# A transformer block's three FFNs: the gate and up products as Strassen's seven quarter products

## The reference, cut to what matters

```python
FFN_HIDDEN = -(-8 * D_MODEL // (3 * 256)) * 256          # 2816

def swiglu(h, w_in, w_out):
    gate, up = jnp.split(h @ w_in, 2, axis=-1)
    return (jax.nn.silu(gate) * up) @ w_out
```

## Time and profile before

| | |
|---|---|
| median of 3 runs | 1612.1 us |
| span of the profiled execution, first to last instruction | 1607.1 us |
| median less this span (what lies around it, and the difference of executions) | 5.0 us |
| TensorE busy | 1596.4 us, 99% |
| VectorE busy | 849.0 us, 53% |
| ScalarE busy | 502.5 us, 31% |
| mean granted TensorE clock | 0.997 |

### The profile page before, as it was taken

One profiled execution on the slowest core, in us unless ns is written; L12 is line 12 of the kernel. 1 busy time (PEld: TensorE's weight loads), 2 busy tenths in 40 slices (PEclk: granted clock), 3 DMA queues, 4 the chain that ended last, 5 costly groups with the idle time before them and its releaser, 6 DMA issues.

```text
span 1607.1 us, 19314 instructions
## 1 busy us (share of the span) xinstructions
PE 1596.4 (99%) x7785; PEld 1343.6 (84%) x7785; DVE 849.0 (53%) x1050; ACT 502.5 (31%) x589; POOL 119.9 (7%) x106
## 2 busy tenths in 40 slices
PE   9999999999999999999999999999999999999998
PEld 7888888888888888888888888888988888888887
DVE  5898764664433344584454444346456544444444
ACT  4554375522222233442222223221323222222222
POOL 0100000020000000000000003135006000000000
PEclk9999999999999999999999999999999999999999
DMA  9544511222222123322222223342212322222332
GB/s 388 193 156 159 208 53 53 80 79 96 87 104 104 66 89 98 116 79 105 99 84 104 91 73 105 98 146 103 80 53 79 105 104 94 89 104 69 95 100 77
DMA packets 30647, 171.35 MB, mean 107 GB/s; under 512 B 3200, under 2 KB 5504, under 8 KB 17152
## 3 DMA queue, kind: packets, MB, share of 16 engines
q1 hardware_dynamic: 26240, 153.80, 27.4%
q0 software_dynamic: 4352, 16.78, 3.1%
HBM read 168.47 MB, written 2.10 MB: 106 GB/s over the span
## 4 chain that ended last, share of the span: by engine, by line
PE 99%; issue 0%; DVE 0%; POOL 0%; ACT 0%; POOLq 0%; DVEq 0%
PE bank L515 98%; PE bank L814 0%; PE bank L870 0%; POOL root L420 0%; PE bank L738 0%; PE bank L1143 0%; DVE y_ffn L2534 0%; ACT tmp L1500 0%; POOLq L123 0%; DVE qd L2111 0%; DVE kd L2111 0%; DVE tmp L2091 0%; DVE y_ffn L2532 0%; ACT mod_rows L1289 0%; DVEq L123 0%
## 5 line engine op out<-in xcount | busy, mean ns | idle before, releaser
L515 PE MATMUL bank<-a_hi,w_all 128*128 128x512 f32 x2490 | 764.7, 390 | 0.0
L515 PEld LDWEIGHTS bank<-a_hi,w_all 128*128 128x128 f32 x2490 | 466.5, 188 | 98.8 <-issue 2.5
L1712 DVE TENSOR_TENSOR w_all<-w_raw,w_all 128x2048 fp32r<-128x2048 f32 x140 | 323.3, 2309 | 360.5 <-ACT w_all L1265 360.3
L515 PE MATMUL bank<-a_lo,w_all 128*128 128x512 f32 x1245 | 477.1, 389 | 0.0
L1265 ACT ACTIVATE w_all<-w_raw 128x2048 fp32r<-128x2048 f32 x142 | 271.7, 1913 | 562.7 <-PE bank L515 562.7
L515 PE MATMUL bank<-g_hi,w_all 128*128 128x512 f32 (+1 forms) x1088 | 331.9, 386 | 0.0
L515 PEld LDWEIGHTS bank<-a_lo,w_all 128*128 128x128 f32 x1245 | 233.7, 188 | 48.8 <-issue 0.5
L515 PEld LDWEIGHTS bank<-g_hi,w_all 128*128 128x128 f32 x1088 | 203.9, 189 | 41.2
L515 PE MATMUL bank<-g_lo,w_all 128*128 128x512 f32 (+1 forms) x544 | 210.2, 386 | 0.0
L515 PEld LDWEIGHTS bank<-g_lo,w_all 128*128 128x128 f32 x544 | 102.5, 188 | 20.6
L515 PE MATMUL bank<-w_all,a_hi 128*128 128x512 f32 (+1 forms) x384 | 108.9, 359 | 0.0
(11 more groups left out here) (289 smaller groups left out, 1339.3 us busy)
## 6 DMA issues: line engine op xcount, KB each, us to landing
w_raw<-in_ffn_in SPq DMA_DIRECT2D x66, 1024.0 KB, 4.8
w_raw<-in_ffn_out SPq DMA_DIRECT2D x24, 768.0 KB, 4.2
mod_raw<-in_mod POOLq DMA_DIRECT2D x16, 1024.0 KB, 5.6
w_raw<-in_ffn_out SPq DMA_DIRECT2D x24, 640.0 KB, 3.9
w_raw<-in_gla_in SPq DMA_DIRECT2D x10, 1024.0 KB, 5.1
w_raw<-in_mix_in SPq DMA_DIRECT2D x10, 1024.0 KB, 4.7
mod_w<-in_mod SPq DMA_DIRECT2D x8, 1024.0 KB, 18.4
w_raw<-in_gla_out SPq DMA_DIRECT2D x4, 1024.0 KB, 4.7
```

The lines of the kernel that those rows point to most:

```text
L515: return pe.matmul(out, lhs, rhs, start=first, stop=last, skip_group_check=True)
L1712: V.tensor_tensor(flat(w_lo[s]), flat(w_raw[s]), flat(w_hi[s]).bitcast(F32), ALU.subtract).then_inc(lo_done[s], 1)
```

## The change

In each FFN the first pair stays as it was. Pairs 2 to 11 (called pairs 1 to 10 of the combined form below, n = 1 to `LAST` = 10) are computed as seven quarter products in place of eight (Strassen's block product in the form with shared sums). The depth of 1024 is cut into two halves, the 256 columns of a unit into two chunks of 128, the 512 tokens into two halves of 256. A quarter product is 128 features x 256 tokens over a depth of 512; gate and up are done side by side in one bank. Seven sums of weight quarters (slots 0 to 6, three of them plain quarters, four by VectorE: `weight_first_two`, `weight_second`, `weight_fourth`) meet seven sums of token quarters (`xc`, made once per FFN, four by VectorE: `token_sums`). Each slot is split into upper and lower part (`weight_hi` on ScalarE, `weight_lo` on VectorE, 128 x 1024 each), each token sum likewise (`token_hi`, `token_lo`). The tokens are scaled by the norm's gains and roots before the sums (`tokens`).

TensorE does the seven products in the order of `STEPS`, 24 matmuls of 256 columns each. Products 0, 2 and 4 build up bank 0, and ScalarE copies the bank after each (`part_copy`) before the next may add to it; product 1 goes to bank 1, 3 and 6 to bank 2, 5 to bank 3. VectorE adds copy and bank to each quarter of gate and up (`quarter_sum`, four per pair; product 6 waits for the first of them), ScalarE applies Silu, VectorE multiplies (`hidden_product`). The hidden values' upper and lower parts are made later, at the end of the last pair and in the first quarter of the output stage.

The loads fill one raw buffer `w_pair` (2 MB for gate and up) by halves of the depth, 1 MB each: the first half for pair n+1 when four lower parts of pair n are done, the second when all seven are.

The diff's core (renamed semaphores, memory places and repeated forms left out):

```diff
+STEPS = ((0, 0, True), (6, 1, True), (5, 0, False), (1, 2, True), (4, 0, False), (2, 3, True), (3, 2, False))
...
+                for n in range(1, LAST + 1):
+                    before = N_STEPS * (LAST * f + n - 2)
+                    for half in range(2):
+                        if n > 1:
+                            sp.wait_ge(combo_lo, before + (4, N_STEPS)[half])
+                        w = slice(half * UNIT // 2, (half + 1) * UNIT // 2)
+                        to = w_pair[:, :, KD // 2 * half:KD // 2 * (half + 1)].rearrange("p u k c -> p u (k c)")
+                        sp.dma_start(to, w_in[CPU * n:CPU * (n + 1), :, w].rearrange("u p w -> p u w")).then_inc(half_in[half], 16)
...
+                def combined(first=False):
+                    for n, (x, b, begins) in enumerate(STEPS):
+                        pe.wait_ge(combo_lo, cnt.next(combo_lo))
+                        if first:
+                            pe.wait_ge(x_lo, cnt.next(x_lo))
+                            if n == 0:
+                                pe.wait_ge(gate_free, cnt.next(gate_free, CPU))
+                            if n == 3:
+                                pe.wait_ge(up_free, cnt.next(up_free, CPU))
+                        if n in (0, 2, 4) and (n or cnt.has(part_copied)):
+                            pe.wait_ge(part_copied, cnt.next(part_copied) if n else cnt.now(part_copied))
...
+                        if n == N_STEPS - 1:
+                            pe.wait_ge(c_added, cnt.next(c_added))
+                        for u in range(CPU):
+                            out = bank[b][:, u * TC:(u + 1) * TC]
+                            for k in range(KD // 2):
+                                m = mm3(out, (slot[n][:, 0, u, k], slot[n][:, 1, u, k]), (xc_hi[:, k, x], xc_lo[:, k, x]),
+                                        begins and u == 0 and k == 0, k == KD // 2 - 1)
...
+                def first_combined():            # ScalarE
+                    for which in range(3):
+                        part_copy(f, 1, which)
+                        weight_hi(f, 1, 4 + which)
+                        token_hi(f, 4 + which)
+                    weight_hi(f, 2, 0)
+                    gate_silu_of(f, 1, 1)
+                    for j in (1, 2, 3):
+                        weight_hi(f, 2, j)
+                    gate_silu_of(f, 1, 0)
+                    for j in (4, 5, 6):
+                        weight_hi(f, 2, j)
+                def combined(n):                 # ScalarE
+                    part_copy(f, n, 0)
+                    weight_hi(f, n + 1, 0)
+                    weight_hi(f, n + 1, 1)
+                    part_copy(f, n, 1)
+                    weight_hi(f, n + 1, 2)
+                    weight_hi(f, n + 1, 3)
+                    part_copy(f, n, 2)
+                    weight_hi(f, n + 1, 4)
+                    gate_silu_of(f, n, 1)
+                    weight_hi(f, n + 1, 5)
+                    weight_hi(f, n + 1, 6)
+                    gate_silu_of(f, n, 0)
...
+            def weight_first_two(f, n):          # VectorE
+                i = LAST * f + n
+                dve.wait_ge(half_in[0], ONCE + 16 * i)
+                V.tensor_tensor(quarter(4, n), raw_quarter(0, 0), raw_quarter(0, 1), ALU.subtract).then_inc(early_sums, 1)
+                dve.wait_ge(early_sums, 2 * i - 1)
+                dve.wait_ge(half_in[1], ONCE + 16 * i)
+                V.tensor_tensor(raw_quarter(0, 1), raw_quarter(0, 1), raw_quarter(1, 1), ALU.add).then_inc(early_sums, 1)
...
+                def combined(n):                 # VectorE
+                    weight_lo(f, n + 1, 0)
+                    weight_first_two(f, n + 1)
+                    weight_lo(f, n + 1, 1)
+                    weight_second(f, n + 1)
+                    weight_lo(f, n + 1, 2)
+                    weight_lo(f, n + 1, 3)
+                    quarter_sum(f, n, 1, 1)
+                    quarter_sum(f, n, 1, 0)
+                    weight_lo(f, n + 1, 4)
+                    quarter_sum(f, n, 0, 0)
+                    weight_lo(f, n + 1, 5)
+                    weight_fourth(f, n + 1)
+                    hidden_product(f, n, 1)
+                    quarter_sum(f, n, 0, 1)
+                    weight_lo(f, n + 1, 6)
+                    hidden_product(f, n, 0)
+                def last_combined():             # VectorE
+                    for k in range(CPU):
+                        hidden_lower(f, k)
+                    split_lo(0, width(0))
+                    quarter_sum(f, LAST, 1, 1)
...
+                weight_lo(f, 1, 0)
+                weight_lo(f, 1, 1)
+                if f == 1:
+                    dve.wait_ge(roots_copied, cnt.next(roots_copied))
+                elif f == 2:
+                    x_roots(5, False)
+                tokens()
+                token_lo(f, 0)
+                if scaled:
+                    first_gate()
+                token_lo(f, 1)
+                first_combined()
```

More of the change, by code:

```diff
@@ L935, in ahead_products @@
                     pe.wait_ge(ahead_lo, at + 1)
-                    m = mm3(bank[b][:], weights(0, k, 0), (g_hi[:, at], g_lo[:, at]), first and i == 0, last and k == AHEAD[-1])
+                    m = mm3(bank[b][:], weights(0, k, 0), (g_hi(at), g_lo[:, at]), first and i == 0, last and k == AHEAD[-1])
                 return m
@@ new lines, in quarter_sum @@
+            def quarter_sum(f, n, c, half):
+                i = LAST * f + n - 1
+                to = cbuf[:, :, c, HALVES[half]]
+                which, b, after = {(1, 1): (2, 2, 4), (1, 0): (2, 1, 2), (0, 0): (0, 3, 6), (0, 1): (1, 2, 7)}[c, half]
+                dve.wait_ge(part_copied, 3 * i + which + 1)
+                dve.wait_ge(product_out, N_STEPS * i + after)
+                if cnt.has(hidden):
+                    dve.wait_ge(hidden, cnt.now(hidden))
+                V.tensor_tensor(to, dec_k[which][:].rearrange("p (u t) -> p u t", u=CPU),
+                                bank[b][:].rearrange("p (u t) -> p u t", u=CPU), ALU.add).then_inc(c_added, 1)
```

617 lines of the change are left out of this document (375 added, 242 removed).

## The result

| | median of runs | ratio to before, 95% interval |
|---|---|---|
| before | 1610.5 us (1608.0 to 1613.7) | |
| after | 1676.1 us (1675.6 to 1677.2) | 1.0406, 1.0388 to 1.0425 |

The change costs 4.1%. The forecast was 1662 us, slower with a chance of 0.88. The direction and the mechanism came out as forecast; the time is 14 us longer. By spans it is 1674.5 against 1607.1: 67.4 us more, where 50.6 were forecast. The 5.0 us that the forecast added between span and median came to 1.6.

The account below looks back on a forecast made before the run. TensorE, busy 99% of the span, was taken to bound the kernel. Span 1607.1 - 48.0 saved + 98.6 of added waits = 1657.7, plus 5.0 to the median gives 1662 us; costs give 1650 to 1690, widened to 1632 to 1700.

Parts of the forecast that it names:

- The 5.0 us that the forecast added: Whole time: the median of runs lies 5.0 us above the profiled span, so this was added to 1657.7.
- TensorE's saving: Combined pairs: 20.16 us in place of 21.76 at 0.120 us per 256-column matmul, 48.0 us saved over 30 pairs.
- not some 99: Whole changed profile: TensorE idle some 99 us, named after VectorE's lower parts and a ScalarE bank copy.
- (a): Ahead of product 0 of pair 1: TensorE waits for work piled on VectorE, 4.8, 9.8 and 11.3 us per FFN.
- (b): Within pair 1: weights and token sums are split while TensorE works on it; waits 7.5, 9.8 and 9.8 us.
- (c): Within pair 2: product 2 waits 11.2 us for ScalarE's first copy of bank 0; 13.3 per FFN with later products.
- (d): Within pair 10: product 6 waits 1.85 us per FFN, as VectorE splits output weights ahead of the quarter sum.
- a load of 6.0 as its upper bound: Half loads in 4 KB rows to two places: taken as 4.8 us; at 6.0 the forecast grows by 24.
- nothing to spare: Pairs 3 to 9: the raw buffer loop takes 19.9 to 20.1 us, just under TensorE's 20.16.
- The second rival: Steady pairs: the raw buffer loop binds, 1 us more per pair in 24 to 27 pairs, 1680 to 1700; chance 0.13.
- I count nothing: Half clock behind the larger waits: priced at zero, since another wait follows that TensorE reaches anyway.
- the third rival: Behind the four larger waits per FFN: half-clock stretches, none hidden, cost 12 x 1.7 = 20 us, 1683; chance 0.10.

Follow-up runs that it names:

- rows_8k: Kernel after with each half load of a combined pair's weights in one 8 KB row per partition in place of two of 4 KB: 1664.5 us, 1.0336.
- rephase: Kernel after with the weight operations of pair n moved behind the sums of pair n-1, beside pair n itself instead of a pair ahead: 1628.3 us, 1.0110.
- plain_second: rephase with the second pair of each FFN also done plain, so 27 combined pairs in place of 30: 1577.0 us, 0.9788.
- copy_early: Kernel after with ScalarE's first copy of bank 0 in pair 2 issued right behind the upper part of slot 1: 1674.3 us, 1.0390.
- sum_early: Kernel after with VectorE's first quarter sum in pair 10 put ahead of its split of the first output unit: 1669.1 us, 1.0366.
- filled_waits: Kernel after with matmuls whose results nobody reads run in the four long waits of each FFN: 1678.5 us, 1.0421.

## Why the prediction was right, and what it mis-sized

TensorE's saving came out in its size: matmuls of 256 columns are spaced 0.120 us, a pair without waits takes 20.16 us (rows_8k, rephase). The waits stand where they were said to be, though the longest are named after the gate's banks and after copies, not after `slot` and `xc_lo`. TensorE idles 76.7 us more than before, not some 99, and is busy 1587.1 us in place of 1548: part of the lost time is work at half clock.

(a) The forecast had 25.9 us, the trace has 23.7 by the same row of VectorE. plain_second shows it causally: with 21.8 us of plain products beside the token work nearly all of it goes.

(b) The first FFN's product 6 starts 24.8 us behind product 0, as forecast; in the others 29.0 and 28.9 in place of 27.1, by the half clock behind product 2 (see below). Product 6 itself then takes 4.1 to 5.3 us, partly at half clock, in place of 2.9. That is why pair 1 is 2.3 to 3.1 us longer than forecast and pair 2 up to 1.8 shorter: the second pair's end is set by VectorE and the loads. From product 6 of pair 1 to the end of pair 2 it is 36.9, 36.7 and 37.4 us, where 36.3 were forecast.

(c) 8.7 to 9.5 us before product 2, where 11.2 were forecast; the half clock of product 6 takes part of it. The mechanism stands, but the name in the text was only its last link: "ScalarE's row has all seven upper parts of pair 2 ahead of the first copy" is true and can be undone without any gain (copy_early). What holds is the phase, weights of n + 1 ahead of the sums of n (rephase: -36.5 us in pair 2, -48 with the loop and (d) together).

(d) As forecast, 1.8 us three times.

The load. The forecast took 4.8 us from rows of 8 KB and gave a load of 6.0 as its upper bound. The page has 5.2 for the two rows of 4 KB, and rows_8k brings it back. That is 5.4 us in pairs 3 to 9; the prediction's mark for them, not over 20.5 us, was kept in the mean (20.42) and passed by a few pairs (up to 20.64). The prediction's sentence that the loop has "nothing to spare" was the right warning. The second rival came in by a fifth of the size it was given.

The clock. "I count nothing" is the term that was mis-sized most: it held for a part of the stretches, and the others cost some 12 us, where the third rival had 20.

Between product 0 and product 2 of pair 1 it held. This takes 9.2 us in the first FFN and 10.8 in the others, in the kernel after, copy_early, sum_early, rows_8k, filled_waits and rephase, at a granted clock anywhere from 0.67 to 1.00.

Behind product 2 of pair 1 it did not hold in the second and third FFN. The first 8 us from the start of product 2, in the second FFN of the kernel after, the third of rows_8k and the second of filled_waits:

```profile
756.46:764.46 8.00, 8.00 (x45) 8.00 (x46) 6.98 (x9) 4.24 (x5) 0.00 (x0) 0.63 0.40 133
...
1318.56:1326.56 8.00, 8.00 (x54) 8.00 (x55) 7.84 (x10) 4.24 (x5) 0.00 (x0) 0.79 0.37 131
...
756.71:764.71 8.00, 7.72 (x62) 7.54 (x63) 7.93 (x10) 4.25 (x5) 0.00 (x0) 1.00 0.41 131
```

From product 2 to product 6 it is 18.2, 17.0 and 16.0 us in these three. In the second and third FFN of the same six kernels, twelve places, it goes by the clock in the same way: 16.0 to 16.1 us at a clock of 1.00, 17.0 at 0.79 or 0.80, 18.1 to 18.2 at 0.62 to 0.64. So the kernel after loses 2.1 us in each of these two FFNs.

Outside of the combined pairs the traces before and after run nearly the same matmuls, and they drift apart only in stretches at half clock. Three of these, each before and then after the change: in the first mixer, in the first FFN's norm and in the second FFN's norm.

```profile
178.60:182.20 3.60, 3.52 (x21) 3.21 (x22) 3.56 (x4) 0.74 (x2) 0.00 (x0) 1.00 1.03 418
178.80:182.40 3.60, 3.60 (x13) 2.87 (x12) 2.49 (x2) 0.00 (x0) 0.00 (x0) 0.53 1.01 383
...
321.00:327.90 6.90, 6.90 (x49) 6.90 (x48) 5.62 (x13) 1.29 (x2) 3.51 (x3) 0.75 0.00 0
322.10:329.00 6.90, 6.90 (x35) 6.90 (x35) 4.99 (x11) 0.17 (x1) 3.26 (x4) 0.51 0.00 0
...
691.60:698.40 6.80, 6.80 (x30) 5.63 (x31) 6.46 (x13) 1.45 (x2) 1.21 (x2) 0.75 0.43 154
707.80:714.70 6.90, 6.90 (x24) 6.03 (x24) 5.54 (x11) 0.72 (x1) 1.41 (x2) 0.51 0.49 135
```

The first two bring the first pair's end 3.1 us later (353.0 in place of 349.9), the third costs 1.6. The fourth stands behind the wait on the roots in the third FFN, which lies in the midst of the up unit. There no second wait takes it up at once:

```profile
1296.50:1301.50 5.00, 5.00 (x10) 3.28 (x11) 2.25 (x4) 0.60 (x1) 0.00 (x0) 0.50 0.00 0
```

These 5 us at 0.50, the lower level of 1.2 GHz, behind a wait of 3.53 us cost 2.5 us of work (2.8 with what is left behind them), and the matmuls that spread the roots, which VectorE waits for, took 2.07 us for two in place of 1.02. The four together are 7.5 of the 7.9 us outside of the pairs; the rest is the difference between the matmuls' starts and their modelled ends.

Only the fourth is shown to come from the change, by its wait. The first three stand in work that the change hardly touches, and kernels with the same work there have them or not: sum_early is without the one in the mixer and ends the first pair 1.6 us earlier than the kernel after; rephase is without it, has half of the second, as the kernel before, and ends the first pair at 350.0. The runs of the kernel before differ in the same sense, from 1608.6 us at a mean clock of 0.997 to 1613.9 at 0.994. Its traced execution was one of the fast ones: a time lies about 1.8 us above its own span, and the rest of the 5.0 us that the forecast added was the distance from this execution to the median. Whether the change makes such stretches more frequent is open, with one trace of the kernel before and no experiment on them.

The rule of the Trainium skill ("TensorE: Matmul & The Clock Gate", section "The HAM clock gate") that an idle TensorE falls back to 1.2 GHz is borne out here by windows at 0.50 behind waits of 3.5 to 9.6 us. What such a stretch costs depends on where it lies, as the rows above show.

So the forecast missed the span by 16.8 us in these terms: -2.2 in (a), +3.7 up to product 6 of pair 1 (half clock behind product 2), +1.9 from there to the end of pair 2, +5.5 for the load in pairs 3 to 9, and +7.9 outside, nearly all half clock. Part of this is luck: (a) and the 5.0 us went the other way, and without them the time would have been some 19 us over the forecast, not 14.

## What to carry to other kernels

A cheaper form of the products pays only where something covers its preparation: count the operations between the last plain product and the first of the new form on each helper engine, and keep as many plain products behind them. Here one more plain pair costs 1.6 us of TensorE's work per FFN and returns 17 net (rephase to plain_second). When a wait has a row of work behind it, moving the instruction that it names moves only the name; ask what phase the row is in, and whether the next stage's preparation has to stand ahead of this stage's results.

## What the runs showed that I had not expected

A 1 MB load of two rows of 4 KB per partition, from two places in DRAM, lands after 5.2 us, of one row of 8 KB from one place after 4.8, in the same kernel and order. At a loop that the forecast gave 0.1 us of slack this is worth 0.26 us in each of 21 pairs, and in the order of plain_second nothing.

TensorE's half clock lowered the mean granted clock of the span from 0.997 to 0.967, by which it could have lost up to some 50 us (an estimate: 0.030 of 1674.5); some 12 us of it show in the time. A stretch at half clock between products 0 and 2 of pair 1 costs nothing, since product 2 waits for another engine anyway; one behind product 2 costs 1.0 us where the clock of the next 8 us is 0.79 and 2.1 where it is 0.63. Filling the waits with matmuls that nobody reads removed some of these stretches, made a new one, and gained nothing in the whole.
